# Alternating token order for the moving operand of split products in a two-layer encoder trunk

## The reference

```python
# layer 0
x = x + even_mixer(rmsnorm(x, e_norm), e_w_in, ..., e_w_out)   # 2048 -> 6160 columns; 2048 -> 2048
x = x + sq_relu_mlp(rmsnorm(x, f_norm[0]), f_w1[0], f_w2[0])   # 2048 -> 8192 -> 2048
# layer 1
x = x + conformer_conv(rmsnorm(x, o_norm), o_pw1, ..., o_pw2)  # 2048 -> 4096; 2048 -> 2048
x = x + sq_relu_mlp(rmsnorm(x, f_norm[1]), f_w1[1], f_w2[1])
return rmsnorm(x, final_norm)

def sq_relu_mlp(h, w1, w2):
    a = jax.nn.relu(h @ w1)
    return (a * a) @ w2
```

## Time and profile before

| | |
|---|---|
| median of 3 runs | 2392.33 us (2388.43 to 2392.42) |
| span of the profiled execution | 2390.7 us |
| median less that span | 1.6 us |
| TensorE busy | 2321.1 us, 97% |
| VectorE busy | 1548.9 us, 65% |
| ScalarE busy | 976.9 us, 41% |
| mean granted TensorE clock | 0.991 of full speed |

### The profile page before, as it was taken

The page is one execution under the profiler, slowest core; times in us unless marked ns, Lnnn a source line. Parts: engine busy times, 40 slices in busy tenths (PEclk is TensorE's granted clock), DMA queues, the critical chain, the costliest instruction groups (busy, mean ns, idle before and its releaser), DMA issues.

```text
span 2390.7 us, 36015 instructions
## 1 busy us (share of the span) xinstructions
PE 2321.1 (97%) x14110; PEld 2066.8 (86%) x14110; DVE 1548.9 (65%) x1809; ACT 976.9 (41%) x1042; POOL 11.5 (0%) x25
## 2 busy tenths in 40 slices
PE   7999998999999999999999999899999999999996
PEld 7988898999888888888888888788888888888885
DVE  7666657467655555555664999977655655655665
ACT  5534344344444444444442100254444444444453
POOL 0000000000000000000000000000000000000000
PEclk9999999999999999999999999999999999999998
DMA  5423234344555554555554444244545555455552
GB/s 216 177 106 115 89 106 124 133 159 181 190 194 178 191 189 180 193 181 188 190 180 141 157 144 155 88 155 180 194 178 191 187 182 193 179 189 186 184 185 112
DMA packets 55863, 396.84 MB, mean 166 GB/s; under 512 B 6496, under 2 KB 6880, under 8 KB 8544
## 3 DMA queue, kind: packets, MB, share of 16 engines
q1 hardware_dynamic: 54288, 389.32, 45.2%
q0 software_dynamic: 1488, 6.29, 1.0%
HBM read 393.49 MB, written 2.10 MB: 165 GB/s over the span
## 4 chain that ended last, share of the span: by engine, by line
PE 79%; DVE 13%; issue 4%; ACT 2%; DMA 1%; DVEq 0%; ACTq 0%; SPq 0%; POOL 0%
PE ps L1013 41%; PE ps L1015 21%; DVE work L908 4%; PE ps L1040 3%; PE ps L988 3%; PE ps L992 3%; PE ps L990 3%; DVE wlo L563 3%; PE ps L1099 2%; DMA raw<-in_wts 1%; ACT whi L262 1%; DVE sq_part L602 1%; PE ps L1164 0%; PE ps L1163 0%; PE ps L1166 0%
## 5 line engine op out<-in xcount | busy, mean ns | idle before, releaser
L563 DVE TENSOR_TENSOR wlo<-raw,whi 128x1024 fp32r<-128x1024 f32 x672 | 820.8, 1224 | 593.1 <-ACT whi L262 579.9
L262 ACT ACTIVATE whi<-raw 128x1024 fp32r<-128x1024 f32 x672 | 709.4, 1060 | 827.4 <-PE ps L1015 559.3
L1013 PE MATMUL ps<-hid,whi 128*128 128x512 f32 x2304 | 813.0, 398 | 3.0 <-DVE hid L941 3.0
L1013 PE MATMUL ps<-xg,whi 128*128 128x512 f32 x2048 | 719.8, 394 | 3.8 <-ACT sq_part L307 3.2
L1015 PE MATMUL ps<-hid,wlo 128*128 128x256 f32 x2304 | 646.9, 281 | 0.0
L1015 PE MATMUL ps<-xg,wlo 128*128 128x256 f32 x2048 | 579.2, 283 | 0.0
L1013 PEld LDWEIGHTS ps<-hid,whi 128*128 128x128 f32 x2304 | 432.7, 188 | 110.1 <-issue 3.7
L1013 PEld LDWEIGHTS ps<-xg,whi 128*128 128x128 f32 x2048 | 384.7, 188 | 93.3 <-ACT sq_part L307 3.5
L1015 PEld LDWEIGHTS ps<-hid,wlo 128*128 128x128 f32 x2304 | 435.3, 189 | 0.0
L1015 PEld LDWEIGHTS ps<-xg,wlo 128*128 128x128 f32 x2048 | 385.0, 188 | 0.0
L988 PE MATMUL ps<-xg,whi 128*128 128x256 f32 x768 | 227.4, 296 | 12.1 <-DVE wlo L563 12.1
(11 more groups left out here) (203 smaller groups left out, 1471.8 us busy)
## 6 DMA issues: line engine op xcount, KB each, us to landing
raw<-in_wts SPq DMA_DIRECT2D x368, 1024.0 KB, 4.8
x<-in_xt SPq DMA_DIRECT2D x4, 512.0 KB, 8.1
x<-in_xt POOLq DMA_DIRECT2D x1, 2048.0 KB, 8.7
out_t<-work POOLq DMA_DIRECT2D x4, 512.0 KB, 3.3
work<-in_rows POOLq DMA_DIRECT2D x12, 128.0 KB, 4.1
ct<-in_consts SPq DMA_DIRECT2D x1, 768.0 KB, 6.4
work<-in_w_s POOLq DMA_DIRECT2D x4, 128.0 KB, 4.6
dwt<-in_dw SPq DMA_DIRECT2D x1, 248.0 KB, 5.1
```

What stands on the lines that cost most here:

```text
L262: nc.scalar.activation(whi[:, i % SPLIT].rearrange("p a b -> p (a b)"), raw[:, r, HALF * (i % 2):HALF * (i % 2) + HALF], ACT.Copy).then_in ...
L563: tt(wlo[:, i % SPLIT].rearrange("p a b -> p (a b)"), raw[:, i // 2 % RAW, HALF * (i % 2):HALF * (i % 2) + HALF], whi[:, i % SPLIT].rearra ...
L1013: mm(ps[:, 4 * par + n, :], whi[:, r, k, cols], operand[:, kt].rearrange("p a t -> p (a t)"), start=(kt == 0), stop=False)
```

## The change

The moving operand of every split product is read in another order of tokens. Before, tokens 0, 1, 2, ... 255 come one after another. Now the two halves of the 256 tokens take turns: 0, 128, 1, 129, ... 127, 255. In memory each read is 128 float32 words (512 bytes) away from the one before. The products of 512 columns do so for the high part and then for the low part. PSUM is still written in the order in which the columns come, so token 128h + i of a tile stands at place 2i + h. VectorE's reads of these sums put the tokens back: they read places 0, 2, 4, ... 254 and then 1, 3, ... 255. `leave_psum` reads both of its operands so, PSUM and `cross`. ScalarE's copy from PSUM to `cross` keeps the order in PSUM and is as before.

```diff
+        def woven(tokens):
+            return tokens.rearrange("p (h i) -> p i h", h=TT)
+        def woven_parts(parts):
+            return parts.rearrange("p a (h i) -> p a i h", h=TT)
+        def in_order(sums):
+            return sums.rearrange("p n (i h) -> p n h i", h=TT)
+        def halves(ap):
+            return ap.rearrange("p n (h i) -> p n h i", h=TT)
...
@@ leave_psum
-                tt(total[:], ps[:, 4 * par:4 * par + 4, 0:T], cross[:], ALU.add).then_inc(banks_free, 1)
+                tt(halves(total[:]), in_order(ps[:, 4 * par:4 * par + 4, 0:T]), in_order(cross[:]),
+                   ALU.add).then_inc(banks_free, 1)
@@ products
-                return ps[:, NARROW_BANK[G]:NARROW_BANK[G] + 2, :].rearrange("p b (n t) -> p (b n) t", t=T)
+                return in_order(ps[:, NARROW_BANK[G]:NARROW_BANK[G] + 2, :].rearrange("p b (n t) -> p (b n) t", t=T))
@@ one of its four readers
-                tt(padded[:, :, 3:3 + T], products(G), by_token(rms[:], 4), ALU.mult).then_inc(banks_free, 1)
+                tt(halves(padded[:, :, 3:3 + T]), products(G), halves(by_token(rms[:], 4)), ALU.mult).then_inc(banks_free, 1)
@@ narrow_group
-                            mm(dst, whi[:, r, k, cols], operand[:, kt, 0, :], start=(kt == 0 and n % 2 == 0), stop=False,
+                            mm(dst, whi[:, r, k, cols], woven(operand[:, kt, 0, :]), start=(kt == 0 and n % 2 == 0), stop=False,
                                skip_group_check=True)
-                            mm(dst, whi[:, r, k, cols], operand[:, kt, 1, :], start=False, stop=False,
+                            mm(dst, whi[:, r, k, cols], woven(operand[:, kt, 1, :]), start=False, stop=False,
                                skip_group_check=True)
-                            ins = mm(dst, wlo[:, r, k, cols], operand[:, kt, 0, :], start=False, stop=(kt == KT - 1),
+                            ins = mm(dst, wlo[:, r, k, cols], woven(operand[:, kt, 0, :]), start=False, stop=(kt == KT - 1),
                                      skip_group_check=True)
@@ group
-                            mm(ps[:, 4 * par + n, :], whi[:, r, k, cols], operand[:, kt].rearrange("p a t -> p (a t)"),
+                            mm(ps[:, 4 * par + n, :], whi[:, r, k, cols], woven_parts(operand[:, kt]),
                                start=(kt == 0), stop=False)
-                            ins = mm(ps[:, 4 * par + n, T:2 * T], wlo[:, r, k, cols], operand[:, kt, 0, :],
+                            ins = mm(ps[:, 4 * par + n, T:2 * T], wlo[:, r, k, cols], woven(operand[:, kt, 0, :]),
                                      start=False, stop=(kt == KT - 1))
```

More of the change, by code:

```diff
@@ L650, in qkvz @@
                 if t0 >= 24:
-                    ins = tt(acts[:, t0:t0 + 4, :], products(G), by_token(rms[:], 4), ALU.mult)
+                    ins = tt(halves(acts[:, t0:t0 + 4, :]), products(G), halves(by_token(rms[:], 4)), ALU.mult)
                     ins.then_inc(banks_free, 1)
@@ L818, in _ @@
                     dve.wait_ge(s["uv_ready"], G - G_UV)
-                tt(total[:], products(G), by_token(rms[:], 4), ALU.mult).then_inc(banks_free, 1)
+                tt(halves(total[:]), products(G), halves(by_token(rms[:], 4)), ALU.mult).then_inc(banks_free, 1)
                 dve.wait_ge(banks_free, G + 3)
@@ L828, in _ @@
                 w = x[:, 4 * j:4 * j + 4, :]
-                tt(w, w, products(G), ALU.add).then_inc(banks_free, 1)
+                tt(halves(w), halves(w), products(G), ALU.add).then_inc(banks_free, 1)
                 dve.wait_ge(banks_free, G + 3)
```

## The result

The changed kernel takes 2285.33 us (2283.25 to 2287.13, 4 runs) against 2391.30 us: a ratio of 0.9555, with a 95% interval of 0.9542 to 0.9569. It is 4.5% faster.

The account below looks back on a forecast made before the run. TensorE was taken as the bound nearly everywhere, through its split products: 2390.7 + 1288 (pairs) + 295 (narrow products) - 25 (mixer idle) + 3 (VectorE reads) = 3952, so 3953 us against the runs' median; range 2388 to 4130 us.

Parts of the forecast that it names:

- Term 1: TensorE's hopping read of the moving operand in split products: pairs add 1288 us, narrow products 295 us.
- full rate: Rival, chance 0.32: TensorE reads both in-line streams without loss, a pair stays at 0.352 us, time 2392 to 2406 us.
- half rate: Likeliest case, chance 0.46: TensorE takes a column per 0.833 ns in split products; time 3873 to 4127 us.
- One support of half rate: TensorE's plain fp32 products (L1040) were read as taking 0.216 us for 256 columns each at full clock.
- The other support: TensorE's first fp32r products at the 1.2 GHz level start 0.21 us apart for 256 columns.
- The row from VectorE: L602's sum of squares, hopping 260 words each element, costs 1.76 ns an element; taken as upper bound for TensorE's column.
- The mixer: Of 36.5 us of TensorE idle there, 25 us between products would vanish under longer products: -25 us, bounds 0 and -60.
- Term 2: VectorE's sum reads stepping two words, in `leave_psum` and narrow groups: 0 to 0.73 us more each; +3 us taken, 14 at most.

Follow-up runs that it names:

- the stretches: Behind the changed kernel's last product, 32 more TensorE products in each of several reading orders, other engines idle: 512 columns take 226 ns in line, 216 two ways.
- the second kernel of stretches: The changed kernel with sixteen sets of 32 further products in other orders behind its last one: 512 columns took 216 to 461 ns; plain fp32 was included.
- the two whole kernels after them: The changed kernel with tokens read 0 4 1 5 2 6 3 7 and sums left unordered: 2282.09 us; with one stream in steps of two words: 4116.47 us.

## Why the prediction was wrong

**What bounds the kernel** was right: TensorE, nearly everywhere, so that the cost of a column goes straight into the time.

**Term 1 failed, at its lower bound.** "Below it is nothing: ... no row shows a reason for a gain" was wrong. The prediction added 0.296 us to a pair and 0.096 us to a narrow product; measured, a pair lost 0.024 us and a narrow product 0.007. The row was in the text: the step from 256 to 512 columns costs 0.44 ns a column where the clock allows 0.417, and a pair 32 ns more than its 0.320. The prediction read this as proof that the read had no slack and so as evidence against full rate. It was the loss that could be won back: 24 ns a pair in MLP 0, 0.352 to 0.328, times 2048 is the 49 us there. The low-clock rows had it too: at 1.2 GHz 256 columns take 0.21 us, a period each, and at 2.4 GHz 0.12 instead of 0.107. So at the high clock something beyond the count of columns took time, and the stretches show that it was the order of reading.

**The choice of half rate** went by a count of hops in the whole stream. The stretches show that a hop is not what costs; the rate falls by half when each of two readers finds one word in a line (0.452 us for 512 columns, and 4116 us in the whole kernel). In the order of the change each finds four. The rival "full rate" came nearest, with its reason (two streams, each in line) nearly the right one: lines kept for any two streams would have made runs of two cheap as well, and these cost 339 ns. Its time of 2392 to 2406 took today's rate for full rate.

**One support of half rate** was misread. The 0.216 us between starts of L1040 is not a product. The trace has 1024 records of that line for 8 groups of 64 products, two for each, just as the last two stretches of the second kernel of stretches have 64 records for 32 products. By these records an fp32 product of 256 columns takes 2 x 0.216 = 0.43 us. The row shows half rate for one record and a quarter for a product, and it says nothing of a read that hops. The other support, 0.21 us for 256 columns at the low clock, is 256 columns at 1.2 GHz and says nothing of a read either.

**The row from VectorE** (L602) was no guide to TensorE. It takes four places in turn, and for TensorE four ways are slow (284 ns) and two are fast. For VectorE too a hop has no such price by itself: two places in turn cost it 1263 ns for 1024 elements, against L602's 1951.

**The mixer.** The 25 us of idle time that were to vanish belonged to a slower TensorE. With a faster one, idle time grew from 36.5 to 45.8 us, so that of 3072 x 7 ns = 22 us saved in products (0.120 us before, 3.5 / 31 = 0.113 for 256 columns in two ways by themselves) only 8.6 reached the end of the stage: busy time fell by 17.8 us and idle time took 9.3 of that. Part of the 4 us missing in busy time is the clock: from 46 to 165 us the granted clock was 0.95 to 0.99 in the changed kernel and 1.00 before, and at 46 us its products start 0.21 us apart where they took 0.12.

**Term 2** was right in its wide bounds and in its cover. The stepped read costs 228 ns, within 0 to 730, and nothing measurable of it is on the path. That the step in PSUM is free and the one in SBUF is not was not foreseen.

**What stays open.** That TensorE's moving operand is fetched by two readers in turn is a model. It gave the rates of six orders before they were run, one of them 2 ns off; the times of the two whole kernels after them follow from rates that the stretches had already measured, and test the model no further. No trace shows the readers, and another mechanism with the same rates is not excluded. It does not say why four ways (284 ns) and runs of two (339) are both better than one word to a line (452), nor why the in-line rate differs with the place (0.116 to 0.123 us for 256 columns), nor why plain fp32 loses in two ways.

## What to carry to other kernels

Compare the distance between dense products with columns over clock; where it is several per cent too long at the high clock (here 0.352 us for 0.320) and exact at the low one (0.21 us for 256 columns), look at the order in which the moving operand is read. For fp32r an order in which words 1, 3, 5 and words 2, 4, 6 each run on in line (two halves in turn, or 0 4 1 5 2 6 3 7) takes the excess away, while a step of two words doubles the time of a product; plain fp32, tried in these two orders only, is better in line. Putting the result back in order while reading PSUM in steps of two costs neither VectorE nor ScalarE anything; in steps of two in SBUF it cost VectorE 228 ns a read, which was hidden here.

## What the runs showed that was not expected

- An in-line fp32r moving operand does not reach the rate of the alternating one: 226 ns for 512 columns with nothing else running, 216 in two ways.
- A single stream in steps of two words halves the rate (455 ns), four words is hardly worse (461).
- VectorE's read of 1024 sums took 1225 ns with `cross` in line, 1453 in steps of two words and 2021 in steps of four, in the kernels with two and four ways.
